# Latent-attention heads of a two-layer decoder trunk: output blocks scaled by row sums, plain query columns of two heads in one block, rotary ones made once, score rows spread over the steps

## What is computed

```python
# 1024 tokens, 12 heads; QK = 64 plain + 32 rotary columns, V = 64
q = (_rms(c_q, mla_q_norm[j]) @ mla_w_q_up[j]).reshape(b, s, N_MLA_HEADS, MLA_QK)   # rank 768 -> 12 x 96
kv = (_rms(c_kv, mla_kv_norm[j]) @ mla_w_kv_up[j]).reshape(b, s, N_MLA_HEADS, MLA_NOPE + MLA_V)
k = concat([kv[..., :MLA_NOPE], k_rope_h], -1)
q = _rms(q, mla_g_qn[j]);  k = _rms(k, mla_g_kn[j])          # over all 96 columns
q, k = rotary on the last 32 columns of each
o = softmax(causal(q @ k.T * QK**-0.5)) @ v                   # in query blocks
```

## Time and profile before

| | us |
|---|---|
| median of 3 runs (lowest, highest) | 2628.19 (2627.41, 2633.21) |
| profiled execution, its own time | 2629.66 |
| span of its trace | 2627.9 |
| busy in the span: PE / PEld / DVE / ACT / POOL | 2526.2 / 2057.7 / 1739.8 / 1310.6 / 1112.5 |

### The profile page before, as it was taken

One profiled execution on the slowest core, in us unless ns is written; L12 is line 12 of the kernel. 1 busy time (PEld: TensorE's weight loads), 2 busy tenths in 40 slices (PEclk: granted clock), 3 DMA queues, 4 the chain that ended last, 5 costly groups with the idle time before them and its releaser, 6 DMA issues. The chain is left out here.

```text
span 2627.9 us, 37382 instructions
## 1 busy us (share of the span) xinstructions
PE 2526.2 (96%) x12150; PEld 2057.7 (78%) x12150; DVE 1739.8 (66%) x2659; ACT 1310.6 (50%) x2483; POOL 1112.5 (42%) x839
## 2 busy tenths in 40 slices
PE   7999999999999999999989999999899999999999
PEld 6867777667888888888777777778687888888887
DVE  6767787855765666478655377777648665665595
ACT  6567777745433333444655366666545333333443
POOL 2134454311465566555411332332003665565554
PEclk9999999999999999999999999999899999999999
DMA  4111110153222232674302000000242322234843
GB/s 145 45 29 33 33 33 9 33 176 113 81 100 104 100 112 88 228 240 148 107 21 59 14 20 22 21 21 21 83 166 90 116 100 104 100 112 143 285 125 117
DMA packets 182796, 242.76 MB, mean 92 GB/s; under 512 B 31376, under 2 KB 105872, under 8 KB 182672
## 3 DMA queue, kind: packets, MB, share of 16 engines
q1 hardware_dynamic: 182672, 241.19, 27.7%
HBM read 175.60 MB, written 65.54 MB: 92 GB/s over the span
## 5 line engine op out<-in xcount | busy, mean ns | idle before, releaser
L2385 POOL TENSOR_TENSOR l0s_run_lo<-l0s_run,l0s_run_hi 128x512 fp32r<-128x512 f32 (+2 forms) x120 | 143.5, 1195 | 215.6 <-DVE l0s_run_hi L2538 215.6
L477 POOL TENSOR_TENSOR l1f_wd_lo<-l1f_d,l1f_wd_hi 128x512 fp32r<-128x512 f32 x77 | 108.0, 1403 | 104.6 <-ACT l1f_wd_hi L552 104.6
L477 POOL TENSOR_TENSOR l0f_wd_lo<-l0f_d,l0f_wd_hi 128x512 fp32r<-128x512 f32 x77 | 109.3, 1422 | 97.2 <-ACT l0f_wd_hi L552 97.0
L84 PE MATMUL banks<-l1f_T_hi,l1f_op_hi 128*128 128x512 f32 x352 | 137.1, 390 | 1.1 <-DVE l1f_T_lo L697 1.1
L84 PE MATMUL banks<-l0f_T_hi,l0f_op_hi 128*128 128x512 f32 x352 | 137.1, 390 | 1.0 <-DVE l0f_T_lo L697 1.0
L85 PE MATMUL banks<-l0f_T_lo,l0f_op_hi 128*128 128x512 f32 x352 | 137.0, 389 | 0.0
L85 PE MATMUL banks<-l1f_T_lo,l1f_op_hi 128*128 128x512 f32 x352 | 136.9, 389 | 0.0
L86 PE MATMUL banks<-l1f_T_hi,l1f_op_lo 128*128 128x512 f32 x352 | 136.9, 389 | 0.0
L86 PE MATMUL banks<-l0f_T_hi,l0f_op_lo 128*128 128x512 f32 x352 | 136.9, 389 | 0.0
L439 POOL TENSOR_TENSOR l1f_s<-l1f_raw 128x512 f32<-128x512 f32 x44 | 66.6, 1513 | 158.1 <-DMA l1f_raw<-in_w_ffn_gu_dram 135.3
L509 ACT ACTIVATE l1f_op_hi<-l1f_s 128x512 fp32r<-128x512 f32 x88 | 55.2, 631 | 140.4 <-PE banks L86 140.4
(11 more groups left out here) (536 smaller groups left out, 8456.1 us busy)
## 6 DMA issues: line engine op xcount, KB each, us to landing
l0f_raw<-in_w_ffn_gu_dram SPq DMA_DIRECT2D x22, 1024.0 KB, 5.0
l1f_raw<-in_w_ffn_gu_dram SPq DMA_DIRECT2D x22, 1024.0 KB, 4.9
l0f_a_raw<-hidden_rows SPq DMA_DIRECT2D x77, 256.0 KB, 3.9
l1f_a_raw<-hidden_rows SPq DMA_DIRECT2D x77, 256.0 KB, 3.4
hidden_rows<-l0f_hid SPq DMA_DIRECT2D x44, 256.0 KB, 2.0
l0f_d<-in_w_ffn_down_dram SPq DMA_DIRECT2D x44, 256.0 KB, 4.9
hidden_rows<-l1f_hid SPq DMA_DIRECT2D x44, 256.0 KB, 2.0
l1f_d<-in_w_ffn_down_dram SPq DMA_DIRECT2D x44, 256.0 KB, 4.8
```

What stands on the lines that cost most here:

```text
L84: pe.matmul(out, l_hi, r_hi, start=first, stop=False, skip_group_check=True)
L477: pool.tensor_tensor(wd_lo[g % RING][:], held[HELD_AT[DOWN[p][1]]][i][:], as_f32(wd_hi[g % RING][:]), ALU.subtract).then_inc(wd_lo_done, 1)
L2385: pool.tensor_tensor(run_lo[x % NR][:, f:HALF], run[x % NR][:, f:HALF], as_f32(run_hi[x % NR][:, f:HALF]), ALU.subtract).then_inc(run_spli ...
```

## The change

1. **Row sums on the output.** `R` is gone, and `I` is one reciprocal of four sums for each job. `T` waits for the exponents alone. SP stores the 512 reciprocals of a job to DRAM (4 bytes at a time, one partition's four values going to four places 512 bytes apart), loads them back spread over 64 partitions, and `E` on DVE becomes two operations: the addition, which frees the bank, and a multiplication by these scales, which waits for that load.
2. **Plain query columns of two heads in one block.** `q half part`: 2 blocks of 18 products to a pair instead of 4, in two parts of 9. The plain columns of head 0 are scaled by DVE, those of head 1 by ACT with a shift of partitions. The sums of squares come from products whose stationary side is the squares (4 products of 2 columns for each half), so they need no turning.
3. **Rotary columns once.** Three blocks of four heads' 32 rotary columns are made in the opening, 3 x 2 x 18 products of 128x512; DVE multiplies each by two tables, SP stores both results to DRAM, and loads the rows of a pair into its queries, three loads a head. Their sums of squares (`rss`, 6 units of 4 small products) go by DRAM to the pairs as well. Twelve small loads at the start spread the table.
4. **Order.** `plan`, `extras` and `OPENING` are written anew. In `extras` the queries of the next pair now stand at steps 0 to 7, keys and values at 7 to 10, `kturn` at 11 to 17, and nothing at 18 to 23.

The diff, cut to its core (lines of the lists and of what each operation waits for):

```diff
-        (self.scores_made, self.raw_max, self.nmax_done, self.exp_done, self.inv_done, self.rows_done,
...
         def score_up_to(count):
             nonlocal made
             while made < count:
                 exp_up_to(made)
-                row_up_to(made - 1)
                 steps.append(("S", made // 4, made % 4))
                 made += 1
+                if made % 4 == 1 and made > 4:
+                    steps.append(("I", made // 4 - 1))
...
             elif kind == "T":
                 n, j, tau = step
-                pe.wait_ge(self.rows_done, turn * self.ns + 4 * n + 4)
+                pe.wait_ge(self.exp_done, turn * self.ns + 4 * n + 4)
...
-            elif kind == "R":
-                n, i = step
-                s = 4 * n + i
-                one, row = slice(s % 4, s % 4 + 1), self.p[n % self.ring][i]
-                dve.wait_ge(self.inv_done, turn * self.ns + s + 1)
-                dve.tensor_scalar(row[:], row[:], self.rinv[:, one], None, ALU.mult).then_inc(self.rows_done, 1)
+                n = step[0]
+                dve.wait_ge(self.exp_done, turn * self.ns + 4 * n + 4)
+                if n >= 2 or not (isinstance(turn, int) and turn == 0):
+                    dve.wait_ge(self.scale_stored, 16 * (turn * self.nj + n - 1))
+                dve.reciprocal(self.rinv[n % 2][:], self.rsum[n % 2][:]).then_inc(self.inv_done, 1)
...
             elif kind == "E":
                 n = step[0]
                 dve.wait_ge(self.tmp_done, turn * self.nj + n + 1)
+                dve.tensor_tensor(self.o_sum, self.o_ps[n % len(self.o_ps)][0:HD, :], self.o_tmp, ALU.add).then_inc(self.out_done, 1)
+                dve.wait_ge(self.out_done, 1 + turn * self.nj + n + 1)
                 dve.wait_ge(self.stored[n % 2], 16 + 16 * (turn * (self.nj // 2) + n // 2))
-                dve.tensor_tensor(self.o_out[n % 2][:], self.o_ps[n % len(self.o_ps)][0:HD, :], self.o_tmp[:],
-                                  ALU.add).then_inc(self.out_done, 1)
+                dve.wait_ge(self.scale_in[n % 2], 16 * (turn * (self.nj // 2) + n // 2 + 1))
+                dve.tensor_tensor(self.o_out[n % 2], self.o_sum, self.o_scale[n % 2], ALU.mult).then_inc(self.out_scaled, 1)
...
+    def step(self, sp, n, turn=0):
+        self.store_scale(sp, n, turn)
+        self.store_out(sp, n - 2, turn)
+        self.load_scale(sp, n, turn)
...
-    extras = {0: ["q 0 0", "q 0 1"], 1: ["v1", "q 0 2"], 3: ["kv 0"], 4: ["kv 1"], 5: ["kv 2", "ksum 0"],
...
+    extras = {0: ["q 0 0"], 1: ["v1", "q 0 1"], 2: ["ss 0", "rq 0"], 4: ["q 1 0"], 5: ["q 1 1", "qhi 0"], 6: ["ss 1", "rq 1", "wq"],
+              7: ["kv 0", "qhi 1"], 8: ["kv 1", "ksum 0"], 9: ["kv 2", "knorm 0", "qnorm 0"], 10: ["kv 3"],
+              11: ["kturn 0", "ksum 1", "wk"], 12: ["knorm 1"], 13: ["v0"], 14: ["kturn 1", "qhi 2"], 15: ["kturn 2", "qnorm 1"],
+              16: ["qhi 3"], 17: ["kturn 3"]}
...
-    plan = [9, 9, 9, 9, 10, 10, 11, 12, 12, 12, 13, 14, 15, 16, 17, 18, 18, 20, 20, 21, 22, 22, 23, 24, 25]
+    plan = [9, 9, 10, 11, 12, 12, 13, 13, 14, 14, 15, 16, 16, 17, 18, 18, 19, 20, 20, 21, 22, 22, 23, 24, 25]
...
+                elif kind == "rss":
+                    r = 2 * int(n[0]) + int(n[1])
...
+                    for i in range(HT):
+                        last = pe.matmul(bank_of(what, g)[:, 4 * i:4 * i + 4], q_sq[r % 2][:, i * P:(i + 1) * P], fours[:],
+                                         start=True, stop=True, skip_group_check=True)
...
-                    u, part = int(n[0]), int(n[1])
-                    h, half = halves[u]
-                    unit = f"q {u} 0"
+                    half, part = int(n[0]), int(n[1])
+                    unit = f"q {half} 0"
```

466 lines of the change are left out of this document (303 added, 163 removed), and 10 rows, old and new, of tables (OPENING, extras).

## The result

The changed kernel takes 2683.57 us, median of 4 runs (2675.24 to 2690.89), against 2627.80 for the kernel before (2626.83 to 2633.21). The ratio is 1.021, 95% interval 1.0184 to 1.0236. The forecast was 2636, in a range of 2608 to 2650: the side was the likeliest one, the size was wrong by 48 us, and the time lies outside the range. The profiled execution has a span of 2683.5 us, 55.6 more than before.

A forecast was written before the change was run, and what follows sets the result against it. PE was taken to bound the turns and opening by its work, the closing being a chain through DVE and ACT. Opening +23.4, turn 0 +0.5, turns -9, closing -8, tail +0.7 gave +7.6: 2636 us, range 2608 to 2650.

The forecast's parts named there:

- Cost 0 ... SP has few issues in a turn and is not late.: Scale's trip over DRAM: made some ten steps, over 22 us, ahead of its E, so it costs nothing.
- two such trips are under 10 us: Bound on the scale's way out and in, from a load of 768 single 4-byte elements that landed in 3.7 us.
- Turn 0: the weights' reload and the last rotary store, +0.5: Turn 0: these two transfers add 0.5 us, with bounds 0 to 2.
- Rival 3: Scale is late: a trip of 25 us holds 24 Es by 3 us each, 72 us, giving 2708; chance 0.02.
- the clock term: Turns, steps 14 to 16: clock at 0.50 adds some 2 us, 61.1 to 63.1; 62.2 taken between them.
- the hand layout: Turn steps 10 to 18 laid out by engine: five PE waits, 8.75 us together, plus 1.1 for other steps.
- The closing: Closing turn: R's going cuts PE idle by 5 and the clock's loss by 3, -8 us, bounds -3 to -12.
- The opening: Opening: PE's work +21.2 and idle +2.2, from 4.2 to 6.4 us, together +23.4.
- Rival 1: DVE keeps up: turn 56.25 us, a gain of 7.75 in each of five, giving 2606; chance 0.32.
- Rival 2: Waits as listed but the clock stays up: turn 61.1 us, sum +2.1, giving 2630; chance 0.24.
- my reason for part 1: Row products lay beside PE's work in the turns, so R's going is worth something only in the closing turn.
- The range's upper end: 2650 us: no gain in the turns, an opening of +26 and a closing of -3, written as +24.

The follow-up runs named there:

- the two kernels without the slow store: Changed kernel with scale store and load left out, outputs multiplied by ones: 2659.59 us; changed kernel with the store in 16-byte pieces, scales in wrong order: 2662.59 us.
- trips put off: Changed kernel, SP storing job n's scale and then loading job n - 1's, first stores between the rotary ones: 2677.91 us, ratio 1.0189.
- The experiment with fillers: Changed kernel with 26, 14 and 12 unread products of 128x256 at PE's three longest waits in each turn before the closing: 2680.11 us, ratio 1.0179.
- the best order tried: Changed kernel with reordered units and SP transfers, later score row, 16-byte scale store, and E's multiplication on GpSimd instead of DVE: 2636.86 us, ratio 1.003.

## Why the prediction was wrong

**The step that failed first: "Cost 0 ... SP has few issues in a turn and is not late."** The trip's term was 0; without the trip the kernel is 24 us faster, half of the miss of 48, and most of that stands in turn 0. Two errors lie in it. The price was taken from the earlier trace rows, a *load* of 768 elements of 4 bytes in 3.7 us, and put on a *store* of 512, which held SP for 8.7 and 9.7 us there and 7.05 on average over 22 of them. The bound put beside that row, "two such trips are under 10 us", was used up by the store alone; no row shows a store of that kind. And the cover was counted only for the scale's own use, an `E` ten steps later. Behind the store's wait in SP's order stood the rotary stores, the base and the weights, and these were urgent; "Turn 0: the weights' reload and the last rotary store, +0.5" should have asked what SP does ahead of that store. The runs show it from both sides: in whole pieces with the order kept, turn 0 is 64.9; in 4-byte pieces with the order changed, 67.9.

Rival 3 had the mechanism's first half. The Trainium skill, "DMA: Bandwidth & Descriptors", section "Rules for kernel authors", has it that a non-contiguous last dimension becomes a descriptor for each element; the store in pieces of 16 bytes agrees, 1.8 us instead of 8.7. I priced the rival only for a trip of over 22 us that holds `E`, and gave it 0.02. The trip was far shorter than that, and its victims were others: the transfers behind it, and one `E` at the very end, where 3.31 us had no cover.

**The turns: the idle time was right, the clock term was not.** Listed by hand were 9.85 us of idle; measured are 9.95, with the longest waits at the places and with the releasers named (1.95 forecast and 3.22 measured at the score row, 2.85 and 2.36 at the first `V`, 1.5 and 1.89 at the next). That the sums agree so well is partly luck: these three are 1.2 longer together than forecast, and the others 1.1 shorter. The busy time was forecast at 51.25 plus 1.1 for the clock, and is 56.15: the clock's term is 4.9, not 1.1. I priced a single fall behind two of the waits and took half of it; the clock stood at 0.50 to 0.60 for 10 us and fell again behind the third. The earlier trace rows had shown how readily it falls, and half a price for a mechanism in whose favour all the rows speak was the wrong choice. In the two kernels without the slow store a turn is mostly 65.0, with a clock of 0.92 and no fall behind the third wait (1.00 there). But "trips put off", which has the slow store, has one turn of 65.0 at 0.92 as well, beside others of up to 67.0; so that the store brings the longer turns about isn't shown. The experiment with fillers says what the clock was worth: of 4.0 us of PE's time that it gave back, 1.3 reached the turn. The rest of the turn's miss is then DVE's and ACT's chain, which the hand layout had right in its places and not in what a faster PE could gain from it.

**The closing: -8 forecast, -3.5 measured** (41.5 to 38.0 between the same two instructions). The clock did rise, from 0.80 to 0.96, and PE's busy time fell by 4.5, more than the 3 put down for it. But I let idle fall from 8.6 to 3 with the row products gone; it is 9.6. The waits for `R` turned into waits for the exponents and the low parts of the same chain. Removing a link that ends a wait shortens it only to the next link, and that one I had not laid out here as I did for steps 10 to 18.

**The opening: +23.4 forecast, +28.3 measured.** The idle part, +3.5 for +2.2, lies inside the bounds given for it (-3 and +5); PE's work had none. PE's busy time rose by 24.8 instead of 21.2: a `rss` unit takes 1.02 instead of 0.95, which is 0.4 together, and the rest fits a mean clock of 0.93 instead of 0.96. Idle is 7.7 where 6.4 was laid out. The 1.0 ahead of the opening is no cost of the change that the traces show: the heads begin between 1477.2 and 1486.5 in the traces of the changed kernel and its variants, on both sides of the 1482.5 of the kernel before, and the wait of 1.47 for SP in front of them is in the kernel before as well. The 108 rotary products are the change's real price: no edit of an order takes them away.

**The rivals.** Rival 1, a turn of 56.25, would have needed DVE to keep up; the best order tried has 60.7. It was given 0.32 for the argument that ACT and DVE had been rarely late before. That argument was worth little, because PE's own work had hidden them, and that work was what the change took away. Rival 2 (the clock stays up) is refuted by the trace of after and by that of every experiment in the new order, where a turn's clock lay between 0.80 and 0.97. And my reason for part 1, that `R`'s going costs nothing and helps only in the closing, was wrong in both orders: +1.6 a turn in the old, -4 in the new. The range's upper end was also 2 too low by its own terms: +24 on 2628.2 is 2652, not 2650.
